# Two convolution tiles ahead of q, k and v, and three tiles' taps on GpSimd instead of two

## The chip, the cores and the metric

The kernel runs on one core of a Trainium2 chip. The metric is the device time of one execution in microseconds, lower is better. One profiled execution, with its trace, stands behind every row below.

## What is computed

The program is one step of a two-layer trunk over 384 tokens (128 of a prompt, 256 of a sample) of width 1024. Layer 0, the only one that the change touches, multiplies the normalised input by one weight matrix and splits the result in two branches: a gated depthwise convolution with 31 taps over 512 channels, and attention with 8 query heads and 2 key/value heads.

```
def conformer_conv(u, dw_w, dw_b, ln_g, ln_b):
    a, b = jnp.split(u, 2, axis=-1)
    g = a * jax.nn.sigmoid(b)
    y = lax.conv_general_dilated(g, dw_w[:, None, :].astype(g.dtype), (1,), [(CONV_PAD, CONV_PAD)],
                                 dimension_numbers=("NWC", "WIO", "NWC"), feature_group_count=CONV_CH)
    y = layer_norm(y + dw_b, ln_g, ln_b)
    return jax.nn.silu(y)
...
    z = h @ w_in
    u, q, k, v = jnp.split(z, EVEN_SPLITS, axis=-1)
    conv = conformer_conv(u, dw_w, dw_b, ln_g, ln_b)
    q = rms_norm(q.reshape(B, S, GQA_KV_HEADS, GQA_GROUP, HEAD_DIM), q_g)
    k = rms_norm(k.reshape(B, S, GQA_KV_HEADS, HEAD_DIM), k_g)
```

After attention the two branches are multiplied by an output matrix; a feed-forward layer follows, then layer 1 with two attentions and a mixture of eight experts. None of that is edited.

## The kernel before

Every engine has its own instruction list, written out by hand in program order; engines meet at semaphores alone. Three stages of layer 0 matter here.

**The input stage** (up to 124 us in the trace). TensorE multiplies seven weight units of 128x2048: three for q, k and v, then four for the convolution, one per tile `c` of 128 channels. Each weight is split in two parts: ScalarE makes the high part (`Wh`, L937), VectorE the rest (`Wl`, L1850); `step(u)` does that two units ahead. For a convolution tile ScalarE takes a sigmoid of one half (L1151) and VectorE multiplies the other half by it into `cpad` (L2171, `gated` below). While TensorE is at the convolution units, the three token tiles of q and k are normalised: ScalarE squares them, VectorE reduces, scales and rotates them (`rms_item`, `scaled`, `rope`: an "item"). Then TensorE transposes q and k (L1616, L1629), with two adaptive-modulation products ("asides") between.

**Attention of layer 0** (`attend(0)`, L1058 and on): 24 steps `s`, one per head and token tile. A step takes scores on TensorE (L1452), a minimum on VectorE (L2002), the exponential on ScalarE (L1058), a transpose (L1460), a copy on VectorE (L2014) and the product with v (L1472). In steps 0 to 21 it also takes one aside: 1 MB of weights by DMA and 16 matmuls (L1417). Steps 0 to 7 have one key tile, steps 8 to 23 three.

**The convolution's taps.** Each of the four tiles needs 31 taps of 128x414. `CT_V = 2` sets the split: tiles 0 and 1 are taps of VectorE, one `scalar_tensor_tensor` each (L1972), multiply and add at once. Tiles 2 and 3 are taps of two engines: ScalarE makes the product into one of three buffers in `work` (L1021), GpSimd adds it to `yc` (L865); ScalarE waits for the add three taps back. All of these lie in attention: `tap()` is called three times per step on ScalarE and three times on VectorE. After the last step VectorE waits for all taps (`conv_chain`, `conv_chain_p`), and the layer norm of the convolution begins.

Of the kernel before, what the change touches and what calls it, by code (L numbers as in the profile page):

```python
# [13 lines left out]
ALU = mybir.AluOpType  # L14
# [14 lines left out]
CT_V = 2  # L29
# [106 lines left out]
def trunk_step(nc, A, out):  # L136
    ctx = ExitStack()
    with ctx:
# [110 lines left out]
        for l in range(2):  # L249
            w_in, w_out = rows(A[f"l{l}_w_in"]), rows(A[f"l{l}_w_out"])  # L250
            base["in", l] = len(units)
            if l == 0:

                for j in range(QKV0):
                    unit(KD, 256, (0, w_in[:, :, 2 * NC + j * 256:2 * NC + (j + 1) * 256]))
                for j in range(CT):
                    unit(KD, 2 * P, (0, w_in[:, :, j * P:(j + 1) * P]),
                         (P, w_in[:, :, NC + j * P:NC + (j + 1) * P]))
# [461 lines left out]
        def pv_bank(m):  # L720
            return psB[m % 2]

# [102 lines left out]
        def _(pool):  # L825
# [29 lines left out]
            pool.wait_ge(z_ready, 1)  # L855
            pool.dma_start(out[2].rearrange("b s h d -> (b s) (h d)"), zq[:, 0, 512:640]).then_inc(state_out, 16)
            pool.dma_start(out[3].rearrange("b s h d -> (b s) (h d)"), zq[:, 0, 640:768]).then_inc(state_out, 16)

            for n in range(CT - CT_V, CW * (CT - CT_V)):
                w, c = divmod(n, CT - CT_V)  # L860
                k = n - (CT - CT_V)
                dst = yc[:, CT_V + c, :]
                pool.wait_ge(tap_made, n + 1)
                wait(pool, conv_chain_p, k - (CT - CT_V) + 1)
                pool.tensor_tensor(dst, dst, tap_product(n), ALU.add).then_inc(conv_chain_p, 1)  # L865
# [54 lines left out]
        def _(act):  # L920
# [87 lines left out]
            def tap():  # L1008

                n = taps[0]  # L1010
                if n >= CW * (CT - CT_V):
                    return
                taps[0] += 1
                w, c = divmod(n, CT - CT_V)
                src, k = cpad[:, CT_V + c, w:w + COUT], dww[:, w * CT + CT_V + c:w * CT + CT_V + c + 1]
                if w == 0:
                    act.activation(yc[:, CT_V + c, :], src, ACT.Identity, scale=k,
                                   bias=vecs[:, V_DWB + CT_V + c:V_DWB + CT_V + c + 1]).then_inc(tap_made, 1)
                    return
                wait(act, conv_chain_p, n - 3 - (CT - CT_V) + 1)  # L1020
# [27 lines left out]
            def attend(a):  # L1048
# [3 lines left out]
                for s in range(NS):  # L1052
# [8 lines left out]
                    if a == 0:  # L1061
                        for _ in range(3):
                            tap()
# [70 lines left out]

            for j in range(QKV0):
                step(base["in", 0] + j)
            for j in range(CT):
                if j < CT - 1:
                    step(base["in", 0] + QKV0 + j)
                if j < NT:  # L1140
                    act.wait_ge(psB_free, first["in0"]["B"] + NT * QKV0)
                    squares(0, j)
                    qk_root(HD, 10)
                    table_of(ACT.Sigmoid)
                g = first["in0"]["A"] + j
# [1346 lines left out]
```

## Time and profile before

| | us |
|---|---|
| median of 3 runs | 1465.2 (1460.79 to 1467.16) |
| the profiled execution's own time | 1462.53 |
| its span in the trace | 1460.7 |
| first scores of attention to last exponential | 130.09 to 225.11 |
| VectorE taps (62), busy | 62.9 |
| GpSimd adds (60), busy | 73.1 |

The profiled execution lies 2.7 us under the median. Start times below are microseconds from the span's start. A busy engine is not by that alone the one that is waited for; which wait ends last is read from the chain of waits.

### The profile page before, as it was taken

What the parts mean: (1) busy time and instruction counts of PE and PEld (TensorE: products, weight loads), DVE (VectorE), ACT (ScalarE), POOL (GpSimd) and SP (SyncE); (2) the same over time, 40 slices, a digit from 0 to 9 for tenths busy, and PEclk for the clock granted to TensorE, in tenths of its full rate; (3) what the DMA queues carried; (4) which work ended last, traced back from release to release, by engine and by line L of the source; (5) the groups of instructions that cost most, each with busy time, mean ns of one, the idle gap of its engine ahead of it and who ended that gap; (6) DMA issues with size and microseconds to landing.
All of it is one profiled execution on the core that took longest, in us unless ns stands there. A gap on an engine that the chain in (4) does not pass through costs nothing.

```text
span 1460.7 us, 19686 instructions
## 1 busy us (share of the span) xinstructions
PE 1290.0 (88%) x7731; PEld 1131.7 (77%) x7731; DVE 929.4 (64%) x1199; ACT 753.6 (52%) x1076; POOL 230.2 (16%) x188
## 2 busy tenths in 40 slices
PE   4798788899999998895974998999999999999995
PEld 1696456799889986893663788888889898898894
DVE  0556996553434344565568533789688798787776
ACT  2434654543223225314535423677777777777773
POOL 0303870200020012000000011011302203112113
PEclk9999889999999998997985896899999999999998
DMA  9743766233444344311950011499798899898882
GB/s 323 201 138 113 238 227 202 87 117 115 130 144 124 100 149 147 116 66 54 297 170 17 1 57 68 146 345 309 266 332 302 281 330 318 279 332 297 286 290 90
DMA packets 178359, 277.66 MB, mean 190 GB/s; under 512 B 7120, under 2 KB 105192, under 8 KB 178264
## 3 DMA queue, kind: packets, MB, share of 16 engines
q1 hardware_dynamic: 176040, 269.87, 55.9%
q0 software_dynamic: 2224, 6.49, 1.6%
q8 instruction: 64, 1.05, 0.3%
q14 instruction: 31, 0.25, 0.1%
HBM read 274.02 MB, written 2.31 MB: 189 GB/s over the span
## 4 chain that ended last, share of the span: by engine, by line
PE 72%; DVE 16%; ACT 5%; issue 5%; DMA 2%; POOL 0%; DVEq 0%; SPq 0%; ACTq 0%
PE psB L1336 5%; PE psB L1338 5%; PE psB L1337 5%; PE psB L1787 4%; PE psB L1789 4%; PE psB L1788 4%; DVE Wl L2370 3%; PE psA L1787 3%; PE psA L1789 3%; PE psA L1788 3%; PE psA L1336 2%; PE psA L1338 2%; PE psA L1337 2%; PE psB L1417 2%; PE psB L1560 2%
## 5 line engine op out<-in xcount | busy, mean ns | idle before, releaser
L2370 DVE TENSOR_TENSOR Wl<-raw,Wh 128x1408 fp32r<-128x1408 f32 (+2 forms) x144 | 248.5, 1744 | 59.7 <-ACT Wh L1236 58.7
L1850 DVE TENSOR_TENSOR Wl<-raw,Wh 128x2048 fp32r<-128x2048 f32 (+4 forms) x64 | 133.9, 2096 | 141.4 <-ACT Wh L937 141.3
L1236 ACT CAST Wh<-raw 128x1408 fp32r<-128x1408 f32 (+2 forms) x144 | 197.7, 1374 | 32.6 <-PE psA L1789 16.5
L937 ACT CAST Wh<-raw 128x2048 fp32r<-128x2048 f32 (+4 forms) x64 | 110.0, 1724 | 137.6 <-PE psB L1338 65.3
L1787 PE MATMUL psA<-Wh,hTh 128*128 128x352 f32 x360 | 119.8, 333 | 0.7 <-ACT hTl L1242 0.7
L1789 PE MATMUL psA<-Wh,hTl 128*128 128x352 f32 x360 | 117.7, 327 | 0.0
L1788 PE MATMUL psA<-Wl,hTh 128*128 128x352 f32 x360 | 117.3, 326 | 0.0
L1336 PE MATMUL psB<-Wh,hTh 128*128 128x256 f32 (+2 forms) x332 | 101.2, 305 | 12.2 <-DVE kv L1958 4.2
L1337 PE MATMUL psB<-Wl,hTh 128*128 128x256 f32 (+2 forms) x332 | 100.2, 302 | 0.0
L1338 PE MATMUL psB<-Wh,hTl 128*128 128x256 f32 (+2 forms) x332 | 100.1, 302 | 0.0
L865 POOL TENSOR_TENSOR yc<-yc,work 128x414 f32<-128x414 f32 x60 | 73.1, 1251 | 47.1 <-ACT work L1021 47.1
L1336 PEld LDWEIGHTS psB<-Wh,hTh 128*128 128x128 f32 x332 | 68.3, 206 | 14.4 <-DVE Wl L1850 5.5
L1787 PE MATMUL psB<-Wh,mTh 128*128 128x512 f32 x198 | 79.0, 399 | 0.0
L1789 PE MATMUL psB<-Wh,mTl 128*128 128x512 f32 x198 | 78.3, 395 | 0.0
L1788 PE MATMUL psB<-Wl,mTh 128*128 128x512 f32 x198 | 78.2, 395 | 0.0
L1417 PE MATMUL psB<-raw,cpad 128*32 128x256 f32 x768 | 63.3, 456 | 16.3 <-DMA raw<-in_l_ada_w 15.8
L904 POOL TENSOR_TENSOR scr<-scr,work 128x512 f32<-128x512 f32 x9 | 11.7, 1302 | 403.3 <-ACT work L1297 403.3
L1787 PEld LDWEIGHTS psA<-Wh,hTh 128*128 128x128 f32 x360 | 69.4, 193 | 1.7 <-ACT hTl L1242 0.9
L1788 PEld LDWEIGHTS psA<-Wl,hTh 128*128 128x128 f32 x360 | 69.7, 193 | 0.9
L1787 PE MATMUL psB<-Wh,hTh 128*128 128x352 f32 x216 | 69.7, 323 | 0.0
L1789 PE MATMUL psB<-Wh,hTl 128*128 128x352 f32 x216 | 69.6, 322 | 0.0
L1788 PE MATMUL psB<-Wl,hTh 128*128 128x352 f32 x216 | 69.4, 321 | 0.0
(347 smaller groups left out, 3362.4 us busy)
## 6 DMA issues: line engine op xcount, KB each, us to landing
raw<-in_l_moe_w SPq DMA_DIRECT2D x108, 704.0 KB, 5.7
raw<-in_l_ada_w SPq DMA_DIRECT2D x48, 1024.0 KB, 5.4
raw<-in_l_ffn_w SPq DMA_DIRECT2D x28, 1024.0 KB, 5.3
raw<-in_l_moe_w SPq DMA_DIRECT2D x27, 768.0 KB, 6.5
gate_b<-in_l_moe_w SPq DMA_DIRECT2D x18, 768.0 KB, 6.9
gate_b<-in_l_moe_w SPq DMA_DIRECT2D x18, 704.0 KB, 5.7
raw_tail<-in_l_moe_w SPq DMA_DIRECT2D x18, 704.0 KB, 5.2
raw<-in_l_w_in SPq DMA_DIRECT2D x11, 1024.0 KB, 5.6
```

Of the source, the lines that this page charges most:

```text
L865: pool.tensor_tensor(dst, dst, tap_product(n), ALU.add).then_inc(conv_chain_p, 1)
L937: act.copy(hi_of(u), raw_of(u)).then_inc(hi_ready, 1)
L1236: act.copy(half_of(Wh, h), raw_half(h)).then_inc(half_hi, 1)
L1336: pe.matmul(o, sh, mh, start=(k == 0), stop=False)
L1337: pe.matmul(o, sh, ml, start=False, stop=False)
L1338: last = pe.matmul(o, sl, mh, start=False, stop=(k == n - 1))
L1417: last = pe.matmul(aside_bank(d)[CG * q:CG * (q + 1), 0:YN], cpad32[:, k, :], aside_raw(d)[:, k, :], start=(k < NCG), stop=(k >= KD - NCG))
L1787: pe.matmul(o, stat[0][:, k, :], vh, start=(k == 0), stop=False)
L1788: pe.matmul(o, stat[0][:, k, :], vl, start=False, stop=False)
L1789: last = pe.matmul(o, stat[1][:, k, :], vh, start=False, stop=end)
L1850: dve.tensor_tensor(lo_of(u), raw_of(u), hi_of(u).bitcast(F32), ALU.subtract).then_inc(lo_ready, 1)
L2370: dve.tensor_tensor(half_of(Wl, h), raw_half(h), half_of(Wh, h).bitcast(F32), ALU.subtract).then_inc(half_lo, 1)
```

## The change

The convolution's tiles get an order, `CONV = [2, 3, 1, 0]`, and the first two of them (`AHEAD_CONV = 2`) are multiplied ahead of q, k and v. The first is multiplied inside the norm, where the first q unit stood. Taps of tiles 2, 3 and 1 are now all made by ScalarE and added by GpSimd (93 products, 90 adds); VectorE keeps tile 0 alone (31 taps). ScalarE begins its taps in the input stage: six after each of the three q, k and v units, four after each item, two after each transposed q tile, and in attention three per step up to step 8 and two from step 9. VectorE takes two taps per step. GpSimd's two DMAs of keys and values for the output move behind its first 60 adds. The squares of q and k move to another place in `work`, clear of the product buffers.

```diff
-CT_V = 2
+CONV = [2, 3, 1, 0]
+AHEAD_CONV = 2
...
+                for n, c in enumerate(CONV):
+                    for j in range(QKV0) if n == AHEAD_CONV else ():
+                        unit(KD, 256, (0, w_in[:, :, 2 * NC + j * 256:2 * NC + (j + 1) * 256]))
+                    unit(KD, 2 * P, (0, w_in[:, :, c * P:(c + 1) * P]),
+                         (P, w_in[:, :, NC + c * P:NC + (c + 1) * P]))
...
+        p_taps = [(w, c) for w in range(CW) for c in CONV[:2]] + [(w, CONV[2]) for w in range(CW)]
...
                     if a == 0:
-                        for _ in range(3):
+                        for _ in range(3 if s < 9 else 2):
                             tap()
...
+            table_of(ACT.Sigmoid)
+            for n in range(AHEAD_CONV):
+                step(conv_unit(n))
+                gate_of(n)
             for j in range(QKV0):
-                step(base["in", 0] + j)
...
+                step(base["in", 0] + AHEAD_CONV + j)
+                for _ in range(6):
+                    tap()
+            for j in range(NT):
+                act.wait_ge(psB_free, qkv_group(QKV0 - 1, NT - 1) + 1)
+                squares(0, j)
+                qk_root(HD, 10)
+                if AHEAD_CONV + j < CT:
                     table_of(ACT.Sigmoid)
...
+                    gate_of(AHEAD_CONV + j)
+                for _ in range(4):
+                    tap()
...
                 transposed_in(g0 + t, qT0[:, :, t * P:(t + 1) * P])
+                for _ in range(2):
+                    tap()
...
-            norm(0, 0, rows_products(base["in", 0], first["in0"]["B"]))
...
+            norm(0, 0, conv_products)
+            for j in range(1, CT):
+                for q in range(QKV0) if j == AHEAD_CONV else ():
+                    unit_b(base["in", 0] + AHEAD_CONV + q, qkv_group(q, 0), (hTh, hTl))
...
-                if taps[0] < CW * CT_V:
-                    w, c = divmod(taps[0], CT_V)
+                if taps[0] < CW:
+                    w, c = taps[0], CONV[3]
...
                     if a == 0:
-                        for _ in range(3):
+                        for _ in range(2):
                             tap()
```

ScalarE at the end of the input stage, before: item 2's squares (L1128) and root, the last two sigmoids (L1151), then the transposed q tiles (L1133) and the two asides' copies (L1028), up to the table of the exponential.

```order
L1128 ACTIVATE work<-zq 128x640 [waits psB_free]
L956 ACT_TABLE_LOAD
L956 ACTIVATE stats<-stats,cst 128x10 [waits ms_ready]
L948 ACT_TABLE_LOAD
L948 ACTIVATE marks<-cst 1x1
L1151 ACTIVATE hf<-psA 128x384 [waits psB_free,psA_full] x2
L1133 COPY qT<-psT 128x4x128 [waits psT_full,psB_free]
L1028 COPY work<-psB 128x256 [waits spread_full,aside_used]
L1133 COPY qT<-psT 128x4x128 [waits psT_full]
L1028 COPY work<-psB 128x256 [waits spread_full,aside_used]
L1133 COPY qT<-psT 128x4x128 [waits psT_full]
L1133 COPY kT<-psT 128x512 [waits psT_full]
```

The same place now, from item 2's squares (now L1148) on; L1041 are the products, L1153 the transposed tiles, L1048 the asides' copies.

```order
L1148 ACTIVATE work<-zq 128x640 [waits psB_free]
L975 ACT_TABLE_LOAD
L975 ACTIVATE stats<-stats,cst 128x10 [waits ms_ready]
L1041 ACTIVATE work<-cpad,dww 128x414 [waits conv_chain_p] x4
L1153 COPY qT<-psT 128x4x128 [waits psT_full,psB_free]
L1041 ACTIVATE work<-cpad,dww 128x414 [waits conv_chain_p] x2
L1048 COPY work<-psB 128x256 [waits spread_full,aside_used]
L1153 COPY qT<-psT 128x4x128 [waits psT_full]
L1041 ACTIVATE work<-cpad,dww 128x414 [waits conv_chain_p] x2
L1048 COPY work<-psB 128x256 [waits spread_full,aside_used]
L1153 COPY qT<-psT 128x4x128 [waits psT_full]
L1041 ACTIVATE work<-cpad,dww 128x414 [waits conv_chain_p] x2
```

Ten products, each of which waits for an add of GpSimd, now stand between item 2's root and the last transposed tile, and both sigmoids stand earlier.

VectorE around item 2, before: the end of item 2 (L1942 to L1945), then the third and the fourth tile's gating (L2171, two rows each), then the first aside's bias (L1984) and attention's first minima (L2002).

```order
L1942 TENSOR_TENSOR scr<-zq,cst 128x10x32 [waits dve_chain]
L1943 TENSOR_TENSOR scr<-zq,cst 128x10x32 [waits dve_chain]
L1944 TENSOR_TENSOR zq<-zq,cst 128x640 [waits dve_chain]
L1945 TENSOR_TENSOR zq<-zq,scr 128x640 [waits dve_chain]
L2171 TENSOR_TENSOR cpad<-psB,hf 128x128 [waits psB_full,psA_free,z_ready]
L2171 TENSOR_TENSOR cpad<-psB,hf 128x256 [waits dve_chain]
L2171 TENSOR_TENSOR cpad<-psB,hf 128x128 [waits psB_full,psA_free]
L2171 TENSOR_TENSOR cpad<-psB,hf 128x256 [waits dve_chain]
L1984 TENSOR_TENSOR gate_b<-psA,gate_b 128x2x256 [waits gate_bias_in,spread_full,psB_free]
L2002 TENSOR_REDUCE stats<-psA 128x1 [waits psA_full] x2
```

The same place now: the fourth tile's gating (now L2197), and all of item 2 behind it.

```order
L2197 TENSOR_TENSOR cpad<-psB,hf 128x128 [waits psB_full,psA_free,z_ready]
L2197 TENSOR_TENSOR cpad<-psB,hf 128x256 [waits dve_chain]
L1957 TENSOR_REDUCE stats<-work 128x10 [waits squares_made,psB_free]
L1965 RECIPROCAL stats<-stats 128x10 [waits root]
L1978 SCALAR_TENSOR_TENSOR zq<-zq,stats 128x512 [waits dve_chain]
L1983 TENSOR_TENSOR zq<-zq,gains 128x512 [waits dve_chain]
L1978 SCALAR_TENSOR_TENSOR zq<-zq,stats 128x128 [waits dve_chain]
L1983 TENSOR_TENSOR zq<-zq,gains 128x128 [waits dve_chain]
L1991 TENSOR_TENSOR scr<-zq,cst 128x10x32 [waits dve_chain]
L1992 TENSOR_TENSOR scr<-zq,cst 128x10x32 [waits dve_chain]
L1993 TENSOR_TENSOR zq<-zq,cst 128x640 [waits dve_chain]
L1994 TENSOR_TENSOR zq<-zq,scr 128x640 [waits dve_chain]
```

Item 2 has moved from ahead of the last two gatings to behind the last one.

## Rows read from the trace of the kernel before

**Rows 1.** The page: span.

```profile
span 1460.7 us, 19686 instructions
```

**Rows 2.** Busy time, (instructions), granted clock, DMA share by stretch.

```profile
core 0: us, PE busy (x) PEld busy (x) DVE busy (x) ACT busy (x) POOL busy (x), PEclk, DMA share, GB/s
...
92.00:124.00 32.00, 32.00 (x188) 31.89 (x186) 20.96 (x36) 13.80 (x20) 1.08 (x2) 1.00 0.22 71
...
131.50:160.00 28.50, 20.10 (x155) 11.66 (x155) 27.61 (x40) 19.37 (x50) 26.25 (x21) 0.85 0.63 205
160.00:205.00 45.00, 37.98 (x309) 23.23 (x307) 43.72 (x60) 27.03 (x67) 36.85 (x32) 0.88 0.74 240
205.00:232.00 27.00, 24.23 (x203) 17.23 (x202) 17.85 (x31) 13.39 (x35) 9.97 (x9) 0.79 0.77 262
```

**Rows 3.** The chain that ended last, 131 to 232 us, shares by line.

```profile
by line: DVE yc L1972 28.5%; issue 15.7%; PE psB L1417 11.9%; PE psB L1472 7.6%; PE psA L1452 6.2%; DVE stats L2002 4.7%; PE psA L1431 4.6%; DVE PT L2014 4.5%; DVE gate_b L1984 4.1%; PE psT L1460 3.6%; ACT Wh L937 1.9%; DVE work L2057 1.4%;
```

**Rows 4.** Tiles yc and cpad: durations ns min/median/max, first and last start.

```profile
L1972 DVE SCALAR_TENSOR_TENSOR yc<-cpad,dww,yc x60: 633/1299/1459, 131.8 to 217.4; 128x414 f32<-128x414 f32 x60
L865 POOL TENSOR_TENSOR yc<-yc,work x60: 907/1262/1422, 133.8 to 218.9; 128x414 f32<-128x414 f32 x60
...
L1021 ACT ACTIVATE work<-cpad,dww x60: 624/634/643, 133.0 to 217.6; 128x414 f32<-128x414 f32 x60
```

**Rows 5.** GpSimd in order of time: start, us, instructions.

```profile
133.75 27.30 POOL L865 TENSOR_TENSOR yc<-yc,work 128x414 f32<-128x414 f32 x22 [33.96 <-ACT work L1021]
```

**Rows 6.** VectorE's taps of steps with three key tiles, in order of time.

```profile
187.98 2.57 DVE L1972 SCALAR_TENSOR_TENSOR yc<-cpad,dww,yc 128x414 f32<-128x414 f32 x3
...
191.54 3.85 DVE L1972 SCALAR_TENSOR_TENSOR yc<-cpad,dww,yc 128x414 f32<-128x414 f32 x3
...
197.31 2.57 DVE L1972 SCALAR_TENSOR_TENSOR yc<-cpad,dww,yc 128x414 f32<-128x414 f32 x3
```

**Rows 7.** ScalarE's exponentials of steps 0, 9, 15 and 23.

```profile
131.46 0.34 ACT L1058 ACTIVATE work<-psA,stats 128x128 f32<-128x128 f32 x1
...
164.25 0.59 ACT L1058 ACTIVATE work<-psA,stats 128x384 f32<-128x384 f32 x1
...
190.04 0.58 ACT L1058 ACTIVATE work<-psA,stats 128x384 f32<-128x384 f32 x1
...
225.11 0.59 ACT L1058 ACTIVATE work<-psA,stats 128x384 f32<-128x384 f32 x1
```

**Rows 8.** TensorE: the product with v that opens one step's work, late steps.

```profile
205.33 1.08 PE L1472 MATMUL psB<-zq,PT 128*128 128x64 f32 x4 [0.24 <-DVE PT L2014]
...
216.34 0.56 PE L1472 MATMUL psB<-zq,PT 128*128 128x64 f32 x4
...
219.26 0.56 PE L1472 MATMUL psB<-zq,PT 128*128 128x64 f32 x4
...
222.60 0.56 PE L1472 MATMUL psB<-zq,PT 128*128 128x64 f32 x4
...
225.09 0.56 PE L1472 MATMUL psB<-zq,PT 128*128 128x64 f32 x4
```

**Rows 9.** Last gating, last q transposes, first scores, in order of time.

```profile
123.84 0.75 DVE L2171 TENSOR_TENSOR cpad<-psB,hf 128x128 f32<-128x128 f32 x2 [6.79 <-PE psB L1338]
...
128.27 0.66 PE L1616 MATMUL psT<-cst,zq 128*128 128x128 f32 x4
...
130.09 0.49 PE L1452 MATMUL psA<-kT,qT 64*128 64x128 f32 x4 [0.73 <-ACT kT L1133]
```

**Rows 10.** VectorE: first and last instruction of item 1 (ten in all).

```profile
103.01 0.81 DVE L1908 TENSOR_REDUCE stats<-work 128x10 f32<-128x640 f32 x1
...
108.46 0.82 DVE L1945 TENSOR_TENSOR zq<-zq,scr 128x640 f32<-128x640 f32 x1
```

**Rows 11.** Experts' stage: weight split on VectorE, additions on GpSimd, ns min/median/max.

```profile
L2370 DVE TENSOR_TENSOR Wl<-raw,Wh x144: 1216/1626/2726, 927.0 to 1431.5; 128x1408 fp32r<-128x1408 f32 x108, 128x1536 fp32r<-128x1536 f32 x27, 128x1024 fp32r<-128x1024 f32 x9
L904 POOL TENSOR_TENSOR scr<-scr,raw_tail x9: 1263/2556/2569, 990.1 to 1445.5; 128x512 f32<-128x512 f32 x9
```

More of the change, by code:

```diff
@@ L721, in pv_bank, with adds_before @@
             return psB[m % 2]
+        p_taps = [(w, c) for w in range(CW) for c in CONV[:2]] + [(w, CONV[2]) for w in range(CW)]
+        def adds_before(n):
+            return sum(w > 0 for w, _ in p_taps[:max(n, 0)])
         def tap_product(n):
@@ L853, in _ @@
             pool.memset(cpad[:, :, :], 0.0).then_inc(pool_chain, 1)
[L855 to L862, printed above, removed]
+            for n, (w, c) in enumerate(p_taps):
+                if n == AHEAD_CONV * CW:
+                    pool.wait_ge(z_ready, 1)
+                    pool.dma_start(out[2].rearrange("b s h d -> (b s) (h d)"), zq[:, 0, 512:640]).then_inc(state_out, 16)
+                    pool.dma_start(out[3].rearrange("b s h d -> (b s) (h d)"), zq[:, 0, 640:768]).then_inc(state_out, 16)
+                if w == 0:
+                    continue
                 pool.wait_ge(tap_made, n + 1)
-                wait(pool, conv_chain_p, k - (CT - CT_V) + 1)
-                pool.tensor_tensor(dst, dst, tap_product(n), ALU.add).then_inc(conv_chain_p, 1)
+                if w > 1:
+                    pool.wait_ge(conv_chain_p, adds_before(p_taps.index((w - 1, c)) + 1))
+                pool.tensor_tensor(yc[:, c, :], yc[:, c, :], tap_product(n), ALU.add).then_inc(conv_chain_p, 1)
             def add_half(n):
@@ L1970, in tap @@
                     else:
[L1971 removed]
+                        dve.wait_ge(conv_chain, taps[0])
                         ins = dve.scalar_tensor_tensor(out=yc[:, c, :], in0=src, scalar=k, in1=yc[:, c, :],
@@ L2141, in _, with gated_value @@
             norm(0, 0)
+            def gated_value(n):
+                g = conv_group(n)
+                dve.wait_ge(psA_free, first["in0"]["A"] + n + 1)
+                dve.wait_ge(psB_full, g + 1)
+                for at, tok, w in CSEG:
+                    ins = dve.tensor_tensor(cpad[:, CONV[n], at:at + w], psB[g % 3][:, tok:tok + w],
+                                            hf[:, n % 2, tok:tok + w], ALU.mult)
+                    if tok == 0:
+                        link(ins)
+                ins.then_inc(psB_free, 1)
+            dve.wait_ge(pool_chain, 1)
+            for n in range(AHEAD_CONV):
+                step(conv_unit(n))
+                gated_value(n)
             for j in range(QKV0):
-                u = base["in", 0] + j
+                u = base["in", 0] + AHEAD_CONV + j
                 step(u)
                 for t in range(NT):
-                    g = first["in0"]["B"] + NT * j + t
+                    g = qkv_group(j, t)
                     if j < 2:
@@ L2179, in _ @@
             attend(0)
-            while taps[0] < CW * CT_V:
+            while taps[0] < CW:
                 tap()
-            dve.wait_ge(conv_chain, CW * CT_V)
-            dve.wait_ge(conv_chain_p, (CW - 1) * (CT - CT_V))
+            dve.wait_ge(conv_chain, CW)
+            dve.wait_ge(conv_chain_p, adds_before(len(p_taps)))
             nothing().then_inc(ln_in, 1)
```

106 lines of the change are left out of this document (51 added, 55 removed).

## The prediction

> **What bounds the kernel now.** The page comes first: span 1460.7 us [rows 1]. The change touches only what lies between the input stage and the end of attention 0, so the views after it are cut to 92 to 232 us. The busy times by stretch [rows 2] show two regimes. From 92 to 124 us TensorE is busy all 32.0 us of 32, so the input stage is TensorE's, and what other engines do there costs nothing while they keep up. From 131.5 to 205 us VectorE is busy 27.61 of 28.5 and 43.72 of 45 us, TensorE 20.1 and 38.0: attention is VectorE's. The chain of waits agrees, with VectorE's taps as its largest entry at 28.5% [rows 3]. Behind 205 us VectorE falls to 17.85 of 27 and TensorE rises to 24.23, at a granted clock of 0.79 [rows 2]. The tile views say what a tap costs: VectorE's takes 633 ns at best and 1299 in the median; the other sort costs ScalarE 634 ns and GpSimd 907 to 1422, median 1262 [rows 4]. So the two engines slow each other: while GpSimd made 22 adds in a row it needed 1.24 us each [rows 5] against 0.907 at best. In late steps three VectorE taps take 2.57 or 3.85 us, six of them 6.42 where six at 0.633 are 3.80; two steps make six adds, so one add costs VectorE 0.43 us [rows 6].
>
> **Input stage.** The matmuls are the same, in another order; the stage still ends with the last convolution unit at 123.8 [rows 9]. ScalarE's 18 products among the q, k and v units wait at worst for six adds, 7.4 us by 1.24 each, and a unit's split is made two units ahead. A unit of 48 matmuls takes 48 x 32.0/188 = 8.2 us [rows 2], so the slack is about 16 us and I cost this at nothing. If the cover were gone, each late split would cost what it is late.
>
> **The way into attention.** Here I see the price. q, k and v are finished two units, 16.4 us, later, and the three items have only two convolution units to hide behind. Item 1 can't begin before the third tile's gating, near 115.6; it takes from 103.01 to 109.28, 6.3 us [rows 10], so to 122. Item 2 now stands behind the fourth gating, which ends at 123.84 + 0.75 = 124.6 [rows 9]. Clean it would end at 130.9. But ten products stand on ScalarE from item 2's root on, so GpSimd adds beside it. The trace does not show an item beside an add; the nearest row is the experts' split, 1626 ns in the median and 2726 at most, a factor of 1.7 [rows 11], and for taps it is 1299/633 = 2.05 [rows 4]. Eight of its ten instructions multiply or add two tensors in SBUF, as those do; as an estimate that is 4.6 of the 6.3 us. By 1.7 it adds 3.2 us and item 2 ends at 134.1; bounds are 0 and, by 2.05, 4.8. From the last q transposes to the first scores it took 128.27 to 130.09, 1.8 us [rows 9]; two more products and a wait for an add stand in it now, 1.24 us. First scores at 134.1 + 1.8 + 1.2 = 137.1, which is 7.0 us late. ScalarE's own list gives nearly the same: ten products from 125.5 on, of which GpSimd paces seven, with the copies and asides between. Bounds: 4 us late with clean items and adds at 0.907, 10 with factor 2.05 and adds doubled as in [rows 11].
>
> **Attention, steps 0 to 8.** VectorE goes from three taps to two, but ScalarE and GpSimd keep three. Before, exponential 0 to 9 took 131.46 to 164.25, 32.8 us [rows 7]; the first steps were short because GpSimd only began then. Now GpSimd sets the pace from the start: three adds, 27 in all. Bounds are 27 x 0.907 = 24.5 and 27 x 1.24 = 33.5 us. Two of three adds meet a VectorE tap, so I take 3 x 0.907 + 2 x 0.33 = 3.4 us a step, 31 with the start: **1.8 us gained**, between 8 gained and 1 lost.
>
> **Steps 9 to 15.** Before: 164.25 to 190.04, 25.8 us for six steps [rows 7]. Two steps took VectorE 9.3 us (187.98 to 197.31), 6.4 of it taps [rows 6]. With four taps and four adds, 4 x 0.633 + 4 x 0.43 = 4.25, two steps take 7.1; TensorE needs 5.8 at its upper clock (219.26 to 225.09 [rows 8]). I take 7.6 because the two then wait for each other: 3 x 7.6 = 22.8, **3.0 gained**, bounds 0 and 6.
>
> **Steps 15 to 23.** VectorE's 31 taps are over by step 15, GpSimd makes two adds a step (2.5 us). TensorE is left, and its clock decides. Two steps took 5.83 us at the upper clock, 2.4 GHz (219.26 to 225.09), and 11.0 at the lower, 1.2 GHz (205.33 to 216.34) [rows 8]. Before: 190.04 to 225.11, 35.1 us for eight [rows 7]. At 3.3 a step (2.9, and some for the 1 MB of weights a step needs: 262 GB/s was the fastest stretch [rows 2]) eight take 26.4, 8.7 gained. Each step at 1.2 GHz costs 5.5 - 3.3 = 2.2 of it. The granted clock was 0.79 to 0.88 before, that is about a quarter of the time at the lower level; two steps of eight take 4.3 back: **4.4 gained**.
>
> **After the last step** I cost nothing: the two products behind exponential 23 (2 x 0.634 us [rows 4]) lie beside TensorE's last steps; uncovered they would cost 1.3 us. 90 adds against 60 is no bound either: 56 are left at 137 us, at 1.24 they end at 206.
>
> **Sum.** -7.0 + 1.8 + 3.0 + 4.4 = 2.2 us gained. The profiled execution would take 1462.53 - 2.2 = 1460.3; it lies 2.7 under the median of the runs, so I say 1463 beside 1465.2, no change that can be told. A measurement of this kernel tells about 0.5%, 7.3 us, from no change.
>
> **A rule weighed.** The measured pair, one add and one tap side by side, costs 1.24 to 1.30 us [rows 4, 5], less than 0.907 + 0.633 = 1.54 and more than either alone. The Trainium skill (SBUF — State Buffer, Who interferes with whom) says that a VectorE instruction with two inputs in SBUF and a GpSimd instruction that reads SBUF contend for one port pair, an exclusive lock: one fully blocks. The trace agrees that they contend, not that one waits out the other. By the page the sum would be the second rival's below.
>
> **Rivals.**
> *Faster.* TensorE is busier in every step, so its clock stays up: 8.7 instead of 4.4 in the last eight steps; adds shrink nearer 0.907 with fewer taps beside them: 4 instead of 1.8; way in 5 late: 4 + 3 + 8.7 - 5 = 10.7 gained, 1454. For it: the late steps at 2.4 GHz ran without idle time. Against: ScalarE made no products beside the last of them [rows 4].
> *Slower, taking turns.* If add and tap exclude each other wholly, a step 0 to 8 takes 3 x 0.907 + 2 x 0.633 = 4.0, 35.9 in all, 3.1 lost; item 2 waits out eight adds, 7.3 us instead of 3.2, so 11.1 late. -11.1 - 3.1 + 3.0 + 4.4 = 6.8 lost, 1472. Against: the 1.24 above.
> *Slower, the clock.* TensorE has little work between 124 and 134 us. If it then stays at 1.2 GHz in the last eight steps they take 44 us, 8.9 lost: -7.0 + 1.8 + 3.0 - 8.9 = 11.1 lost, 1476. Past 0.5% it decides from 6.3 such steps of eight on (-7.0 + 1.8 + 3.0 + 8.7 - 2.2n below -7.3). For it: 205 to 216 us ran so. Against: that stretch ended by itself.
> *It does nothing.* If the end of attention hung on GpSimd, 30 more adds would lengthen it by 37 us. The second convolution unit ends five units of 8.2 us before 123.8, at 83, so adds begin some 50 us earlier than at 133.75 [rows 5], and I give this no chance of its own.
>
> **How the numbers follow.** Forecast 0.48, faster 0.30, taking turns 0.10, clock 0.12. The likeliest case gives 1463. The range 1452 to 1474 takes in the faster case and the taking of turns and leaves out the clock in full and the far ends. Faster by over 0.5%: 0.30. Slower: the clock and most of the other, 0.20. Same: 0.50.
>
> **What would show it.** Right if first scores come at 135 to 139; item 2's reduction follows the fourth gating; taps on VectorE end by step 15; GpSimd is busy without gaps in steps 0 to 8 at 1.0 to 1.2 us an add; steps 16 to 23 take near 3.3 us with TensorE without idle time. Wrong if the input stage ends later than 124 (a split late behind taps), if scores start by 133, or if late steps hold to 4.4 us.

## The result and the profile after

The changed kernel takes **1449.2 us** (median of 4 runs, 1446.8 to 1453.44) against 1462.99 us (4 runs of the kernel before in the same session): ratio 0.9922, 95% interval 0.9895 to 0.995. That is 13.8 us less by the medians (0.9%) and 0.8% less by the ratio, and outside the predicted range of 1452 to 1474. One execution of six of e11 below took 1887.84 us at a granted clock of 0.627, the others 1444.65 to 1446.45; its ratio leaves that one out. The profiled execution takes 1450.84 us against 1462.53, 11.7 less; its span is 11.7 shorter too, so the working below goes by spans.

The windows of the changed kernel by stretch, columns as in [rows 2]:

```profile
92.00:124.00 32.00, 31.50 (x229) 30.62 (x227) 17.09 (x32) 22.83 (x34) 22.08 (x20) 1.00 0.21 67
124.00:137.00 13.00, 5.86 (x34) 3.04 (x32) 9.92 (x9) 8.62 (x17) 11.65 (x10) 0.72 0.48 159
137.00:168.00 31.00, 24.69 (x185) 14.47 (x183) 24.34 (x40) 22.55 (x58) 28.35 (x26) 0.73 0.61 198
168.00:188.00 20.00, 18.45 (x182) 12.20 (x183) 17.93 (x31) 13.29 (x36) 15.21 (x15) 1.00 0.98 323
188.00:215.00 27.00, 27.00 (x281) 18.87 (x280) 13.03 (x28) 19.34 (x53) 17.95 (x19) 1.00 1.00 324
```

Read downwards, the bound moves. On the way into attention (124 to 137) nothing but GpSimd is near full, 11.65 of 13. In steps 0 to 8 GpSimd leads with 28.35 of 31. From 188 on TensorE is busy all 27.00 us at a granted clock of 1.00 (2.4 GHz), and VectorE is at 13.03. Before, VectorE was busy 15.00 of 15 us in the first part of this stretch, and the clock stood at 0.92 and then 0.75:

```profile
190.00:205.00 15.00, 12.00 (x95) 7.06 (x95) 15.00 (x19) 8.22 (x20) 12.93 (x12) 0.92 0.71 229
205.00:227.00 22.00, 21.76 (x184) 15.09 (x183) 14.87 (x27) 11.15 (x32) 9.97 (x9) 0.75 0.72 233
```

The chain that ended last in the changed kernel, 137 to 222 us, shares by line:

```profile
by line: issue 20.1%; PE psB L1449 17.6%; PE psB L1504 8.7%; PE psA L1459 8.4%; DMA raw<-in_l_w_out 7.4%; PE psA L1484 6.9%; PE psT L1492 5.8%; POOL yc L884 5.3%; PE psA L1463 4.0%; DVE yc L2021 3.2%; PE psT L1517 2.7%; ACT Wh L956 2.2%; DV
```

VectorE's taps (yc L2021) were the largest entry, 28.5% [rows 3], and are 3.2% now; TensorE's lines have taken their place. New in it is the transfer of the output matrix (`in_l_w_out`), 6.31 us behind TensorE's last side product, from 209.51 us on.

ScalarE's exponentials 0, 9, 15 and 23 of the changed kernel, to lay beside [rows 7]:

```profile
137.76 0.34 ACT L1078 ACTIVATE work<-psA,stats 128x128 f32<-128x128 f32 x1
...
168.18 0.59 ACT L1078 ACTIVATE work<-psA,stats 128x384 f32<-128x384 f32 x1
...
188.27 0.59 ACT L1078 ACTIVATE work<-psA,stats 128x384 f32<-128x384 f32 x1
...
213.12 0.59 ACT L1078 ACTIVATE work<-psA,stats 128x384 f32<-128x384 f32 x1
```

The first is 6.3 us late (131.46 before). From there steps 0 to 9 take 30.42 (32.79 before), 9 to 15 take 20.09 (25.79), 15 to 23 take 24.85 (35.07). So 6.3 is lost and 2.4 + 5.7 + 10.2 gained: 12.0 at the last exponential, of which 11.7 reach the end.

Where the 6.3 went: the fourth gating and item 2 on VectorE, the adds beside them on GpSimd, and the last transposes and first scores on TensorE, each in order of time:

```profile
121.76 0.75 DVE L2197 TENSOR_TENSOR cpad<-psB,hf 128x128 f32<-128x128 f32 x2
122.42 0.81 DVE L1957 TENSOR_REDUCE stats<-work 128x10 f32<-128x640 f32 x1
...
124.58 1.43 DVE L1983 TENSOR_TENSOR zq<-zq,gains 128x512 f32<-128x512 f32 x1
126.05 0.89 DVE L1978 SCALAR_TENSOR_TENSOR zq<-zq,stats 128x128 f32<-128x128 f32 x1
...
127.90 1.09 DVE L1991 TENSOR_TENSOR scr<-zq,cst 128x320 f32<-128x320 f32 x1
...
131.90 1.57 DVE L1994 TENSOR_TENSOR zq<-zq,scr 128x640 f32<-128x640 f32 x1
```

```profile
124.18 10.07 POOL L884 TENSOR_TENSOR yc<-yc,work 128x414 f32<-128x414 f32 x8 [0.56 <-ACT work L1041]
```

```profile
133.53 0.65 PE L1665 MATMUL psT<-cst,zq 128*128 128x128 f32 x4 [0.89 <-DVE zq L1994]
...
136.39 0.70 PE L1484 MATMUL psA<-kT,qT 64*128 64x128 f32 x4 [1.78 <-ACT kT L1153]
```

The gating comes 2.1 us earlier than before [rows 9]. But item 2 takes from 122.42 to 133.47, 11.0 us where item 1 of the kernel before took 6.3 [rows 10]; its multiplication of 128x640 goes from 0.82 to 1.57 us. The eight adds beside it take 1.26 us each, and 0.907 at best [rows 4]. The transposes wait for that item and the scores for the transposes.

The 2.1 us of the input stage come from 70 to 81 us. Before, a wait of 1.29 us stood there at 70.35, in front of the second q, k, v unit's products, for VectorE's copy of the first; in the changed kernel a convolution unit follows there, without a wait. TensorE's clock was lower before, too. The wait, and the same window of the kernel before and of the changed one:

```profile
70.35 0.55 PE L1336 MATMUL psB<-Wh,hTh 128*128 128x256 f32 x1 [1.29 <-DVE zq L2150]
```

```profile
70.00:81.00 11.00, 10.65 (x67) 10.68 (x68) 4.00 (x6) 1.05 (x1) 0.00 (x0) 0.72 0.97 239
```

```profile
70.00:81.00 11.00, 11.00 (x66) 11.00 (x65) 4.76 (x6) 4.17 (x4) 0.00 (x0) 0.92 0.89 241
```

### The profile page after: what moved, and what is told of

The parts are those of the page before. It is cut to its first block, busy times and chain, and to the rows that moved or that the text cites. A ratio compares the mean times of both kernels' runs of the same rounds, so it can differ in the third digit from the quotient of the medians.

```text
span 1449.0 us, 19747 instructions
## 1 busy us (share of the span) xinstructions
PE 1280.1 (88%) x7731; PEld 1125.7 (78%) x7731; DVE 904.2 (62%) x1168; ACT 772.7 (53%) x1108; POOL 258.7 (18%) x218
## 4 chain that ended last, share of the span: by engine, by line
PE 70%; DVE 12%; issue 8%; ACT 5%; DMA 2%; POOL 1%; SPq 0%; DVEq 0%; ACTq 0%; POOLq 0%
PE psB L1836 5%; PE psB L1838 5%; PE psB L1837 4%; PE psB L1368 4%; PE psB L1370 4%; PE psB L1369 4%; PE psA L1836 3%; PE psA L1838 3%; PE psA L1837 3%; DVE Wl L2423 3%; PE psB L1449 2%; PE psB L1592 2%; PE psB L1591 2%; PE psB L1593 2%; PE psA L1368 2%
## 5 line engine op out<-in xcount | busy, mean ns | idle before, releaser
L1368 PE MATMUL psB<-Wh,hTh 128*128 128x256 f32 (+2 forms) x356 | 106.6, 299 | 10.9 <-DVE kv L2007 4.2
L884 POOL TENSOR_TENSOR yc<-yc,work 128x414 f32<-128x414 f32 x90 | 101.3, 1148 | 63.8 <-ACT work L1041 61.0
L1369 PE MATMUL psB<-Wl,hTh 128*128 128x256 f32 (+2 forms) x356 | 105.8, 297 | 0.0
L1370 PE MATMUL psB<-Wh,hTl 128*128 128x256 f32 (+2 forms) x356 | 105.8, 297 | 0.0
L923 POOL TENSOR_TENSOR scr<-scr,work 128x512 f32<-128x512 f32 x9 | 11.7, 1302 | 403.7 <-ACT work L1329 403.7
L1368 PEld LDWEIGHTS psB<-Wh,hTh 128*128 128x128 f32 x356 | 71.6, 201 | 13.0 <-DVE kv L2007 5.4
L1369 PEld LDWEIGHTS psB<-Wl,hTh 128*128 128x128 f32 x356 | 71.6, 201 | 0.3
L1370 PEld LDWEIGHTS psB<-Wh,hTl 128*128 128x128 f32 x356 | 71.5, 201 | 0.4
```

Of the source, the lines that this page charges most:

```text
L884: pool.tensor_tensor(yc[:, c, :], yc[:, c, :], tap_product(n), ALU.add).then_inc(conv_chain_p, 1)
L1368: pe.matmul(o, sh, mh, start=(k == 0), stop=False)
L1369: pe.matmul(o, sh, ml, start=False, stop=False)
L1370: last = pe.matmul(o, sl, mh, start=False, stop=(k == n - 1))
```

## The experiments

**Theory 1**: the gain is VectorE's relief. Before, a tap of VectorE and an add of GpSimd lay beside each other in every step, VectorE set the step, and TensorE, waiting, fell to its lower clock; with the taps over at 189 us TensorE works without gaps at 2.4 GHz. **Rivals**: the slow last stretch of before was chance; the order of the matmuls alone does it; adds that begin early do it; or it is the clock by itself. All intervals below lie between exponentials, in us; ratios are to the kernel before in the same session.

| kernel | median | ratio, 95% | first exp. | 0 to 9 | 9 to 15 | 15 to 23 |
|---|---|---|---|---|---|---|
| before | 1462.99 | | 131.46 | 32.79 | 25.79 | 35.07 |
| changed | 1449.2 | 0.9922 (0.9895-0.995) | 137.76 | 30.42 | 20.09 | 24.85 |
| e1, before again | 1457.99 (one run) | | 130.81 | 32.80 | 25.93 | 35.42 |
| e2, order only | 1461.15 | 1.0014 (1.0002-1.0027) | 130.47 | 32.91 | 25.52 | 40.61 |
| e3, split, no early adds | 1464.35 | 1.0045 (1.0029-1.0062) | 131.61 | 37.94 | 26.56 | 35.27 |
| e4, early adds, old split | 1454.84 | 0.998 (0.9959-1.0001) | 139.05 | 35.53 | 24.16 | 25.79 |
| e5, way in cleared | 1445.04 | 0.9896 (0.9875-0.9917) | 131.03 | 31.53 | 21.01 | 24.94 |
| e6, way in filled | 1453.44 | 0.9952 (0.9934-0.9969) | 136.62 | 31.79 | 21.10 | 24.87 |
| e7, before, 7 fillings a step | 1465.43 | 1.0034 (1.0018-1.0049) | 130.62 | 31.13 | 29.42 | 37.61 |
| e8, half the load | 1446.09 (one run) | | 136.58 | 31.40 | 20.24 | 24.85 |
| e9, before, taps dropped | 1442.2 | 0.9891 (0.986-0.9921) | 129.56 | 32.23 | 19.35 | 24.79 |
| e10, before, 3 fillings to step 16 | 1459.32 | 1.0001 (0.9988-1.0014) | 129.31 | 31.26 | 27.25 | 38.36 |
| e11, cleared, 8 products a unit | 1446.09 | 0.9904 (0.9886-0.9922) | 133.11 | 30.96 | 21.20 | 24.79 |
| e12, before, 3 fillings to step 19 | 1460.29 | 1.0018 (0.9999-1.0037) | 131.08 | 31.12 | 27.60 | 32.62 |

**e1, the kernel before once more**, nothing edited.

> The kernel before, unchanged, for a second trace. Theory 1 (the forecast's term for steps 15 to 23 was too small because these steps before were held by VectorE's taps and by TensorE's lower clock, and both went away together): the stretch of lower clock in the late steps need not lie at 205 to 216 us again, but the mean granted clock from 131 to 227 us stays between 0.80 and 0.92, and exponential 15 to 23 takes 33 to 36 us. Rival (the first trace had bad luck with the clock): 30 us or less.

The three intervals come out within 0.4 us of the first profile's, and the granted clock from 131 to 227 us is 0.82 (0.84 in the first). The slow stretch belongs to the kernel; chance is out.

**e2, the order of the units alone**: the changed kernel with the old split, and all products of ScalarE inside attention, three a step.

```diff
-p_taps = [(w, c) for w in range(CW) for c in CONV[:2]] + [(w, CONV[2]) for w in range(CW)]
+p_taps = [(w, c) for w in range(CW) for c in CONV[:2]]
...
-                for _ in range(6):
+                for _ in range(0):
...
-                        for _ in range(3 if s < 9 else 2):
+                        for _ in range(3):
```

> The new order of the convolution tiles alone; the taps as before, 62 of VectorE and 62 products with 60 adds, all inside attention, three and three per step. Theory 1 (the gain is the taps taken out of attention): first scores at 130 to 132 us since item 2 is late but runs clean, attention 94 us as before, 1461 to 1466 us, no change. Rival (the order itself gains, by an input stage that TensorE ends sooner): 1455 or less.

No gain. Its last stretch is even longer, in this window from step 15 on:

```profile
190.00:228.00 38.00, 32.98 (x233) 21.68 (x233) 28.17 (x42) 17.10 (x44) 22.81 (x21) 0.73 0.64 209
```

The clock is 0.73 there, lower than the 0.80 of the kernel before from 190 to 225 us. By the time from the span's start the fourth gating comes at 121.69 to 123.84 us in the six profiles with the old order and at 120.11 to 122.66 in the eight with the new one; these ranges overlap. They part when they are counted from where TensorE goes on behind the norm (67.72 us before, 67.86 in the change): 55.5 to 56.2 us later in all six with the old order, 53.9 in seven with the new (e11, the eighth, is told below). So the earlier end of the input stage belongs to the order. It isn't seen in the time, since item 2, now behind the last gating, takes it back: from the fourth gating to the first scores it took 6.25 us before and takes 8.9 here.

**e3, order and split, but no product before attention** (0 in place of 6, 4 and 2; four a step in attention).

```diff
-                        for _ in range(3 if s < 9 else 2):
+                        for _ in range(4):
```

> The new order and the new split (VectorE 31 taps, GpSimd 90 adds), but no tap ahead of attention: four products per step there. Theory 1: GpSimd becomes the bound, 90 adds at 1.1 to 1.24 us are 99 to 112 us from about 132, so the taps end at 231 to 244 us where the layer norm began at 235 before: 1462 to 1474 us. Rival (VectorE's relief is enough by itself): 1455 or less.

GpSimd, in order of time:

```profile
133.91 32.69 POOL L884 TENSOR_TENSOR yc<-yc,work 128x414 f32<-128x414 f32 x30 [84.58 <-ACT work L1041]
167.31 8.60 POOL L884 TENSOR_TENSOR yc<-yc,work 128x414 f32<-128x414 f32 x8 [0.71 <-ACT work L1041]
176.07 24.57 POOL L884 TENSOR_TENSOR yc<-yc,work 128x414 f32<-128x414 f32 x22 [0.16 <-ACT work L1041]
...
201.72 33.16 POOL L884 TENSOR_TENSOR yc<-yc,work 128x414 f32<-128x414 f32 x30
```

90 adds end at 234.9 with hardly a gap: the new split alone only moves the bound from VectorE to GpSimd. The early start is no ornament, it is what pays for the third tile.

**e4, early adds with the old split**: the early products as in the change, but 60 adds for GpSimd and 62 taps, three a step, for VectorE.

```diff
-                if taps[0] < CW:
-                    w, c = taps[0], CONV[3]
+                if taps[0] < 2 * CW:
+                    w, c = taps[0] // 2, CONV[2 + taps[0] % 2]
...
-                        for _ in range(2):
+                        for _ in range(3):
                             tap()
```

> The new order, products and adds ahead of attention as in the change (36 products, 34 adds), but the old split: VectorE keeps two tiles, 62 taps, three per step, GpSimd 60 adds. Theory 1 (VectorE holds the steps): steps 0 to 8 take 36 to 39 us instead of 30.4, the later ones 3.3 to 3.5 each, 1455 to 1460 us, that is half of the gain. Rival (the adds taken out of attention are all of the gain, since taps without an add beside them take 0.63 us): 1448 to 1452.

This one taught more than it was made for. VectorE's taps of its last part, and the windows around it:

```profile
L2020 DVE SCALAR_TENSOR_TENSOR yc<-cpad,dww,yc x36: 637/642/1449, 173.0 to 217.0; 128x414 f32<-128x414 f32 x36
```

```profile
138.00:174.00 36.00, 28.50 (x182) 16.12 (x180) 34.16 (x47) 22.40 (x56) 31.84 (x27) 0.59 0.54 176
...
199.00:225.00 26.00, 25.31 (x256) 17.36 (x256) 20.62 (x43) 9.60 (x32) 0.00 (x0) 1.00 0.98 320
```

GpSimd is done at 175 us. From then on a tap takes 642 ns in the median instead of 1299 [rows 4], three make 1.9 us a step, and steps 15 to 23 take 25.79 at a full clock, with all of VectorE's taps of these steps still there. So it isn't the number of taps that held the last steps, but the taps beside adds. It loses its gain earlier: steps 0 to 9 take 35.53, with VectorE busy 34.16 of 36 us and the clock at 0.59. Its time can't be told from that of the kernel before (interval 0.9959 to 1.0001).

**e5, the way in cleared**: no products behind item 2's root and the transposes; ten more in attention.

```diff
-                for _ in range(4):
+                for _ in range((4, 4, 0)[j]):
...
-                for _ in range(2):
+                for _ in range((0, 0, 0)[t]):
...
-                        for _ in range(3 if s < 9 else 2):
+                        for _ in range(3 if s < 19 else 2):
```

> The changed kernel without ScalarE's four products behind the third item's root and without the six between the q transposes; the ten come later, by three products a step to step 18 instead of to step 8. Theory 1 (GpSimd's adds beside item 2 are what doubles its multiplies and makes attention begin late): item 2 takes 6.3 to 7 us instead of 11.0, first scores at 130.5 to 132 instead of 136.4, steps 0 to 9 within 1 us of 30.4, and steps 9 to 18 at three adds and a step of 3.3 us at most, so 2 to 5 us less in all, near 1445. Rival (item 2 is slow for another reason, its own instructions or the place it stands at): first scores stay later than 134 and the time is within 2 us of the changed kernel's or above. Second rival (GpSimd becomes the bound once ten more adds stand in attention): first scores come early but steps 9 to 18 take 3.6 us or more and the time is that of the changed kernel, 1449.

VectorE's fourth gating, then of item 2 the reduction, two short multiplications and the last two instructions; then the first scores:

```profile
120.86 0.75 DVE L2197 TENSOR_TENSOR cpad<-psB,hf 128x128 f32<-128x128 f32 x2
121.52 0.81 DVE L1957 TENSOR_REDUCE stats<-work 128x10 f32<-128x640 f32 x1
...
124.40 0.29 DVE L1978 SCALAR_TENSOR_TENSOR zq<-zq,stats 128x128 f32<-128x128 f32 x1
...
125.05 0.49 DVE L1991 TENSOR_TENSOR scr<-zq,cst 128x320 f32<-128x320 f32 x1
...
126.10 0.82 DVE L1993 TENSOR_TENSOR zq<-zq,cst 128x640 f32<-128x640 f32 x1
126.96 0.82 DVE L1994 TENSOR_TENSOR zq<-zq,scr 128x640 f32<-128x640 f32 x1
```

```profile
129.66 0.80 PE L1484 MATMUL psA<-kT,qT 64*128 64x128 f32 x4 [0.73 <-ACT kT L1153]
```

Item 2 takes 6.3 us again (121.52 to 127.78), and the first scores come 6.7 us earlier than in the change, 0.9 of it from an earlier gating. The adds beside item 2 were the price. From the fourth gating to the first scores it takes 8.8 us here, as in e2 and e3, and 14.6 in the change. Of these 5.8 us item 2 makes 4.8; the rest lies behind it, where two products stand ahead of the last transposed tile (2.9 us from the last transposes of q to the scores, 1.8 here).

e5 takes ScalarE's products away together with the adds; item 1 of the changed kernel tells the two apart:

```profile
117.88 2.31 ACT L1041 ACTIVATE work<-cpad,dww 128x414 f32<-128x414 f32 x4
118.59 5.02 POOL L884 TENSOR_TENSOR yc<-yc,work 128x414 f32<-128x414 f32 x4 [4.23 <-ACT work L1041]
```

```profile
118.16 0.49 DVE L1992 TENSOR_TENSOR scr<-zq,cst 128x320 f32<-128x320 f32 x1
118.69 1.50 DVE L1993 TENSOR_TENSOR zq<-zq,cst 128x640 f32<-128x640 f32 x1
```

Beside products alone an instruction keeps its 0.49 us; the next one, beside the first add, takes 1.50 and not 0.82.

The ten products cost 1.1 us in steps 0 to 9 and 0.9 in 9 to 15, so 4.6 are left at exponential 23. The median is 1445.04 (1442.96 to 1447.6) against 1449.2; the two intervals to the kernel before overlap, so that this version beats the change is likely rather than settled.

**e6, TensorE kept busy on the way in**, where the clock falls to 0.72: products nobody reads.

```diff
+            def fill(n, bank):
+                for _ in range(n):
+                    pe.matmul(bank[:, 0:P], ident, ident, start=True, stop=True)
...
                     else:
+                        fill(20, psA[0])
                         aside_spread(EARLY_0 + t - 1)
...
+                        if a == 0 and s < 6:
+                            fill(4, psT[g % 2])
                         pe.wait_ge(psA_free, f["A"] + s + 1)
```

> The changed kernel with matrix products that nobody reads on TensorE wherever it idles between the last convolution matmul and step 5: 20, 10 and 6 of 128x128 on the way into attention and 4 in each of steps 0 to 5. They take nothing out. Theory A (GpSimd's three adds a step set the pace of steps 0 to 9, the lower clock there is hidden): granted clock near 1.00 from 124 to 154 us, but steps 0 to 9 take 29 to 30.4 us and the time falls by 0 to 2 us. Theory B (the lower clock, 0.50 from 138 to 152 us, sets the pace of steps 0 to 4 at 4.4 us each): steps 0 to 9 take 27 us or less and the time falls by 3 to 5 us. Third: the filling stands in the way, and the time rises.

Its windows:

```profile
124.00:132.00 8.00, 7.98 (x72) 6.73 (x70) 7.79 (x7) 4.69 (x9) 8.00 (x8) 1.00 0.50 152
132.00:138.00 6.00, 4.44 (x34) 3.65 (x33) 3.17 (x7) 4.90 (x10) 3.23 (x4) 1.00 0.39 136
138.00:146.00 8.00, 6.87 (x48) 5.68 (x49) 7.31 (x11) 5.80 (x15) 8.00 (x7) 0.79 0.03 6
146.00:154.00 8.00, 8.00 (x86) 5.67 (x84) 7.07 (x11) 5.50 (x13) 8.00 (x8) 1.00 0.90 291
154.00:168.00 14.00, 11.92 (x93) 6.97 (x85) 9.01 (x16) 9.11 (x24) 12.63 (x13) 0.70 0.85 281
```

The clock is 1.00, 1.00, 0.79 and 1.00 in the first four windows, to 154 us, where the change has 0.64, 0.78, 0.50 and 0.53, and steps 0 to 9 still take 31.79: GpSimd, busy 8.00 of 8, sets them, as theory A said, though it put them at 29 to 30.4. The lower clock only comes later, 0.70 from 154 to 168 us. The time is 4.2 us above the change's, as in the third case, in another session and with intervals that overlap (to the kernel before each); 1.3 us of it are seen at exponential 23, the rest is not explained.

**e7, the kernel before with seven unread products a step.**

```diff
+                        if a == 0 and 6 <= s < 22:
+                            fill(7, psT[g % 2])
                         pe.wait_ge(psA_free, f["A"] + s + 1)
```

> The kernel before with 7 matrix products of 128x128 that nobody reads on TensorE in each of steps 6 to 21, where it waits for the exponential; VectorE, ScalarE and GpSimd keep their work. It separates the two parts of what the last eight steps gained. Theory 1 (most of it is the clock: TensorE idle beside VectorE falls to 1.2 GHz, which then outlasts VectorE's taps): granted clock near 1.00, steps 15 to 23 take 28 to 30 us instead of 35.1, the time falls by 4 to 7 us. Rival (it is VectorE's relief alone): the clock is up but steps 15 to 23 still take 33 us or more, and the time is unchanged or, with 1.5 us of filling a step, higher.

```profile
190.00:205.00 15.00, 15.00 (x151) 11.42 (x143) 13.73 (x20) 7.86 (x19) 10.91 (x11) 1.00 0.62 205
205.00:227.00 22.00, 22.00 (x217) 17.97 (x213) 13.87 (x24) 10.49 (x28) 10.16 (x9) 1.00 0.72 225
```

Inconclusive: the clock is 1.00, but the filling itself has made TensorE the bound (22.00 of 22). It was mis-sized.

**e10 and e12, three a step instead**, to step 16 and to step 19 (`6 <= s < 17`, `6 <= s < 20`, `fill(3, ...)`).

> The kernel before with 3 instead of 7 unread products of 128x128 a step on TensorE, in steps 6 to 16 alone: with seven TensorE had no idle time left, so that run could not tell the clock's part from the filling's. Three take 0.87 us, TensorE then has 3.8 us of work in a step of 4.65 that VectorE sets. Theory 1 (the clock that falls beside VectorE's taps costs a good part of the last steps): granted clock near 1.00 from 150 to 215 us, steps 15 to 23 at 28 to 32 us instead of 35.1, 3 to 7 us less in all. Rival (the clock costs nothing by itself, since VectorE sets the pace): steps 15 to 23 at 34 us or more and no change in the time.

> The kernel before with the three unread products a step kept up to step 19 instead of step 16, past the end of VectorE's taps: with the filling over at step 16 the clock fell again right behind it, so that run left open what the clock alone is worth. TensorE has about 3.8 us of work a filled step. Theory 1 (part of the last steps' gain is the clock by itself): granted clock 1.00 from 190 to 225 us, steps 15 to 23 take 30 to 32.5 us instead of 35.1, the time falls by 3 to 5 us. Rival (VectorE's taps beside the adds hold these steps at any clock): clock 1.00, but steps 15 to 23 take 34 us or more.

e10 holds the clock only while it fills: 1.00 from 177 to 205, then 0.69 to 227, and its last steps take 38.36. So it told nothing of them. e12's windows:

```profile
190.00:205.00 15.00, 13.87 (x122) 9.54 (x121) 14.96 (x20) 7.87 (x19) 12.82 (x11) 1.00 0.76 245
205.00:225.00 20.00, 18.68 (x200) 13.75 (x198) 14.36 (x25) 11.43 (x33) 9.63 (x8) 1.00 0.80 256
```

With the clock at 1.00 in both, steps 15 to 23 take 32.62 instead of 35.07: some 2.5 of the change's 10.2 us came with the clock by itself, the filling included. VectorE, busy 14.96 of 15, holds the rest; steps 15 to 18 took 16.6 us before, 16.2 here and 10.6 in the change. The last exponential of the profiled execution comes 2.7 us earlier than before, with 1.7 gained in steps 0 to 9 and 1.8 lost in 9 to 15; the time of all ten executions doesn't fall (1.0018), and the profiled one, 1458.34, is the fastest of them.

**e8, half of the side products' weights not loaded**, which halves the transfers of a step.

```diff
-                sp.dma_start(aside_raw(d), ada_w[l][:, :, u * YN:(u + 1) * YN]).then_inc(aside_landed[d % RING], 16)
+                k = KD // 2 if FRONT + PREP_ASIDES < d < FRONT + EARLY else KD
+                sp.dma_start(aside_raw(d)[:, 0:k, :], ada_w[l][:, 0:k, u * YN:(u + 1) * YN]
+                             ).then_inc(aside_landed[d % RING], 16)
```

> The changed kernel with half of the weights of attention's side products not loaded (the products then read what stands in the buffer), so that a step needs 0.5 MB instead of 1 MB; TensorE's work is the same. Theory 1 (with VectorE relieved TensorE bounds the last steps, 27.00 us busy of 27): steps 15 to 23 stay at 24.9, at least 24.4. Rival (the transfers bound them, DMA share 1.00 at 324 GB/s): steps 15 to 23 take 23.6 us or less, 2.92 us each as the kernel before showed at its upper clock.

```profile
188.00:200.00 12.00, 12.00 (x116) 8.18 (x119) 7.60 (x16) 7.70 (x21) 7.70 (x8) 1.00 0.54 169
200.00:213.00 13.00, 13.00 (x143) 9.07 (x136) 4.83 (x11) 9.76 (x28) 8.64 (x9) 1.00 0.61 185
```

Steps 15 to 23 take 24.85, to the hundredth what they took with the whole load. A DMA share of 1.00 beside a busy TensorE was no bound.

**e9, the kernel before without VectorE's last 34 taps.**

```diff
-                if taps[0] < CW * CT_V:
+                if taps[0] < 28:
```

> The kernel before, whose VectorE makes only the first 28 of its 62 taps (the other 34 are left out, two of the convolution's channel tiles stay unfinished); products, adds, order and everything else as before. It shows VectorE's relief by itself, from step 9 on, without a wider use of GpSimd. Theory 1 (VectorE's taps alone hold the last steps up, and with them gone TensorE keeps its clock): steps 0 to 9 as before, 32 to 33 us; steps 9 to 15 take 19.5 to 21 us and steps 15 to 23 take 24.5 to 26, as in the changed kernel; 14 to 17 us less in all. Rival (it needs the adds over early too, as GpSimd's 60 adds last past step 18): steps 9 to 15 stay at 23 us or more, steps 15 to 23 at 28 or more. A granted clock near 0.8 in the last steps would say that the clock falls without VectorE's help.

```profile
164.00:177.00 13.00, 13.00 (x138) 8.88 (x132) 6.37 (x16) 11.37 (x30) 12.96 (x15) 1.00 0.98 324
177.00:190.00 13.00, 13.00 (x124) 8.51 (x124) 7.12 (x14) 10.15 (x24) 10.84 (x12) 1.00 0.92 296
190.00:205.00 15.00, 15.00 (x161) 10.68 (x160) 6.31 (x14) 10.54 (x31) 10.17 (x11) 1.00 1.09 354
```

This decides it. Steps 0 to 9 stay as they were; from where the taps stop, TensorE is busy without a gap at 1.00, and the two intervals are 19.35 and 24.79, the change's 20.09 and 24.85, with every add of GpSimd still there (GpSimd is busy 12.96 of 13).

**e11, eight products a unit** with the way in cleared, so six adds fewer in attention (the edit against e5).

```diff
-                for _ in range(6):
+                for _ in range(8):
...
-                        for _ in range(3 if s < 19 else 2):
+                        for _ in range(3 if s < 13 else 2):
```

> The cleared way in, with eight products instead of six on ScalarE in each of the q, k and v units, so that 61 instead of 67 adds are left for attention (three a step to step 12, then two). Theory 1 (GpSimd bounds attention once the way in is clear: 67 adds of 1.108 us are 74 of 77.5 us from exponential 0 to 23): steps 9 to 15 fall from 21.0 to 18.5 to 20 us, the rest stays, 1 to 3 us less than with six, near 1443. Rival (TensorE and VectorE hold these steps, or eight products make a split late in the input stage): steps 9 to 15 stay at 20.5 or more, or the fourth gating comes later than 121.5, and the time is 1445 or more.

A miss for my theory of it: steps 9 to 15 stay at 21.20 (21.01 in e5), so GpSimd does not bound them, and the fourth gating comes at 122.66 instead of 120.86, attention 2.1 us later. TensorE's last product of the stage begins at 120.90 here (120.38 in e5). The gating behind it waits for item 1, whose last three instructions, not two, stand beside adds (1.09, 1.43 and 1.57 us). With eight products a unit ScalarE comes late to the items: item 0 waits 2.52 us for its squares, 0.91 in e5.

## Why the prediction was wrong

By its own steps, gains positive, in us of the profiled execution:

| step | predicted | measured |
|---|---|---|
| first scores | 137.1 (-7.0) | 136.39 (-6.3) |
| steps 0 to 8 | +1.8 | +2.4 |
| steps 9 to 15 | +3.0 | +5.7 |
| steps 15 to 23 | +4.4 | +10.2 |
| after the last step | 0 | -0.3 |
| sum | +2.2 | +11.7 |

**The step that failed is "Steps 15 to 23".** The mechanism was right: VectorE's taps nearly over by then (the last at 188.7, step 15), TensorE left. Two sizes in it were wrong. I took 3.3 us a step and charged 4.3 us for two steps at the lower clock, because I read the rows as a quarter of that time at it [rows 2, 8]. (Their 0.79 to 0.88 are 24 to 42% of the time at half the clock, and from 190 to 225 us it was 0.80, or 40%: read rightly, the charge would have been larger still.) Measured were 3.1 a step and no lower clock from 154 us on (1.00 in every window to 215). The clock of before was no property of the stretch to be carried over: TensorE had it while it waited for VectorE. e9 shows that it goes with the taps. This accounts for 5.8 of the missing 9.5.

**Steps 9 to 15** are the second, 2.7 us. I let two steps take 7.6, half a microsecond above VectorE's sum "because the two then wait for each other"; they took 6.7 with VectorE busy 17.93 of 20, that is 6.0 in two steps and not 7.1, and TensorE 18.45. e9's 19.35 says that TensorE holds them.

**Steps 0 to 8** were right, and for the reason given: GpSimd's three adds set them. e6 raised the clock of the first of them and they got no shorter.

**The way into attention** came out by two errors that nearly cancel. The input stage, costed at nothing, ended 2.1 us earlier. From the fourth gating to the first scores the price was then 8.4 (121.76 to 136.39, against 123.84 to 130.09), not 7.0, because item 2 took 11.0 us and not 9.5 (6.3 and 3.2). I took the split's factor of 1.7 on 4.6 us of it [rows 11]. The item grew by 4.8 us, the figure of my upper bound, but by luck, since the loss is no factor: seven of its instructions grew by 0.60 to 0.75 us each, the longest from 0.82 to 1.57, the shortest from 0.29 to 0.89. The cause, adds beside it, is shown by e5.

**The rivals.** "Faster" was the case that came, with 0.30: its 8.7 for the last steps was 10.2. That its sum, 10.7, lies so near 11.7 is in part luck: it had 4 for steps 0 to 8 (2.4), 3 for 9 to 15 (5.7) and 5 late (6.3). Its argument against, that ScalarE made no products beside the late steps of before, was none.

"Taking turns" did not come at its price: steps 0 to 8 took 3.4 us each and not 4.0, and item 2 grew by 4.8 us and not 7.3. As a mechanism it did come. In item 2 eight adds (124.18 to 134.25) and seven of VectorE's instructions follow one another one for one, and each of the seven is longer by nearly the same time, whatever its own: a wait, not a share of the pace. Read one by one, 39 of the 60 taps of the kernel before are stretched; with its own 0.633 us counted back from its end, each of the 39 begins 0.18 to 0.19 us before the add beside it ends (0.13 to 0.14 in item 2). So the prediction's reading, that neither waits out the other because a pair takes 1.24 to 1.30 us and not 1.54, was wrong: a tap waits for the rest of an add that has already begun, 0.67 us in the median, and not for 0.907. The Trainium skill (SBUF — State Buffer, Who interferes with whom) has one engine wait out the other's instruction; this trace agrees, up to these last 0.2 us.

"The clock" did come between 124 and 154 us, but it rose again by itself while TensorE had work.

## What to carry to other kernels

When an engine is relieved, price what stands behind it from rows in which it ran without waiting, clock included, and don't carry the clock of the waiting time over. Two engines that slow each other are best moved out of each other's time: here either the taps or the adds could stay in the last steps (e4, e9), and the adds not beside the chain that leads into the next stage (e5). Where they must meet, count the instructions that meet and not their time: each paid about the same here, so that short ones lost the most for their length. Filling TensorE's idle time to hold its clock is worth little while another engine sets the pace (e6, e12).

## What the runs showed of the hardware

A tap of VectorE takes 0.642 us alone (e4) and about 1.30 beside adds, an add 0.907 at best and 1.26 in the median beside taps. The loss is a wait for each instruction: in item 2 VectorE's multiplications grew by 0.60 to 0.75 us, those of 0.29 us as those of 0.82. Item 2's reduction, which reads one tensor, lies inside four adds (122.42 to 123.23 in 118.59 to 123.61) and takes 0.81 us, as without adds [rows 10]. The transfers of a step, 1 MB in 3.1 us at 324 GB/s and a DMA share of 1.00, could be halved with no effect on steps 15 to 23 (e8). The way in cost nothing by its lower clock: the granted clock was 0.57 from 126 to 154 us in the change and 0.94 in e6, and from the fourth gating to the first scores it took 14.6 and 14.7 us; steps 0 to 9 were no shorter either.
